# Where one vector engine runs its convolution taps: spread over the steps of prompt attention and over other pages of the cached sequences

## What is computed

```python
z = rms_norm(x) @ w_in                       # q latent | kv latent | rotary key | conv input
# group B: latent attention, 8 heads; prompt causal, samples over 16 cached pages + own tokens
# group A: convolution over time, 512 channels, 31 taps
glu = a * jax.nn.sigmoid(g)
xc = jnp.concatenate([conv_state, glu], axis=1)
y = depthwise_conv(xc, conv_w) + conv_b      # y[t, c] = sum_k xc[t + k, c] * w[k, c]
y = silu(layer_norm(y))
x = x + concat(rms_norm(attn), rms_norm(y)) @ w_out
x = x + (silu(h @ w_gate) * (h @ w_up)) @ w_down          # h = rms_norm(x), width 2816
x = x + sigmoid(rms_norm(x) @ w_ple_gate) * (p @ w_ple_proj)
```

## Time and profile before

| | us |
|---|---|
| median of 3 runs (1737.22 to 1741.24) | 1740.86 |
| the profiled execution | 1738.36 |
| its span, first to last instruction | 1736.3 |
| PE busy | 1654.8 |
| DVE busy | 1243.3 |
| ACT busy | 660.2 |
| POOL busy | 525.1 |

### The profile page before, as it was taken

One profiled execution on the slowest core, in us unless ns is written; L12 is line 12 of the kernel. 1 busy time (PEld: TensorE's weight loads), 2 busy tenths in 40 slices (PEclk: granted clock), 3 DMA queues, 4 the chain that ended last, 5 costly groups with the idle time before them and its releaser, 6 DMA issues.

```text
span 1736.3 us, 28852 instructions
## 1 busy us (share of the span) xinstructions
PE 1654.8 (95%) x10632; PEld 1480.8 (85%) x10632; DVE 1243.3 (72%) x1843; ACT 660.2 (38%) x1240; POOL 525.1 (30%) x351
## 2 busy tenths in 40 slices
PE   6999898999999999989998999999999999999998
PEld 6999787677788898877888999999999888887886
DVE  5385887776689889876689777777777577955444
ACT  5302345664444444553443223233222244542111
POOL 2204585420465565541124222222221000700000
PEclk9999999999999999999999999999999999999999
DMA  6401000001242222302103444444444877662011
GB/s 185 148 1 47 15 1 1 1 1 51 60 132 68 67 58 57 89 21 84 49 25 107 166 149 142 140 140 140 140 140 141 285 241 273 200 215 79 31 44 46
DMA packets 156044, 172.89 MB, mean 100 GB/s; under 512 B 35155, under 2 KB 107376, under 8 KB 155805
## 3 DMA queue, kind: packets, MB, share of 16 engines
q1 hardware_dynamic: 153939, 170.52, 30.7%
q10 hardware_dynamic: 2002, 1.03, 0.2%
HBM read 131.06 MB, written 40.80 MB: 99 GB/s over the span
## 4 chain that ended last, share of the span: by engine, by line
PE 74%; DVE 10%; POOL 5%; issue 4%; ACT 3%; SPq 3%; DMA 1%; ACTq 0%; DVEq 0%; POOLq 0%
PE ps L2619 20%; PE ps L2621 20%; PE ps L2620 20%; POOL stats L976 2%; PE ps L3034 2%; PE ps L2860 1%; SPq L761 1%; DVE arena L2184 1%; PE ps L2817 1%; PE ps L616 1%; DVE arena L1789 1%; PE ps L2922 1%; PE ps L2813 1%; PE ps L2819 1%; PE ps L2818 1%
## 5 line engine op out<-in xcount | busy, mean ns | idle before, releaser
L1125 POOL TENSOR_TENSOR arena<-arena,mhalf 128x32 f32<-128x32 f32 x32 | 176.4, 5512 | 130.2 <-DVE arena L2188 130.2
L2619 PE MATMUL ps<-cw_hi,pT_hi 128*128 128x288 f32 x512 | 161.8, 316 | 9.9 <-DVE pT_lo L2076 5.6
L1789 DVE SCALAR_TENSOR_TENSOR arena<-arena,tapw 128x1024 f32<-128x1024 f32 x120 | 161.8, 1348 | 1.5
L2393 DVE TENSOR_TENSOR dn_lo<-dn_raw,dn_hi 128x1024 fp32r<-128x1024 f32 x83 | 116.8, 1416 | 61.6 <-ACT dn_hi L1692 60.7
L2619 PE MATMUL ps<-T_hi,S_hi 128*128 128x272 f32 x528 | 152.7, 289 | 3.7 <-DVE F_B_r L670 1.8
L2620 PE MATMUL ps<-F_B_r,S_hi 128*128 128x272 f32 x528 | 152.3, 288 | 0.0
L2621 PE MATMUL ps<-T_hi,S_lo 128*128 128x272 f32 x528 | 152.0, 288 | 0.0
L2620 PE MATMUL ps<-cw_lo,pT_hi 128*128 128x288 f32 x512 | 150.8, 294 | 0.0
L2621 PE MATMUL ps<-cw_hi,pT_lo 128*128 128x288 f32 x512 | 150.7, 294 | 0.0
L1692 ACT ACTIVATE dn_hi<-dn_raw 128x1024 fp32r<-128x1024 f32 x83 | 87.6, 1060 | 136.0 <-DMA dn_raw<-in_w_down 66.7
L1440 ACT ACTIVATE arena<-ps 128x512 f32<-128x512 f32 x128 | 76.7, 599 | 123.8 <-PE ps L2621 123.7
(11 more groups left out here) (403 smaller groups left out, 4852.7 us busy)
## 6 DMA issues: line engine op xcount, KB each, us to landing
dn_raw<-act_mid SPq DMA_DIRECT2D x77, 256.0 KB, 2.7
arena<-in_cache_ckv SPq DMA_DIRECT2D x128, 128.0 KB, 2.0
dn_raw<-in_w_down SPq DMA_DIRECT2D x45, 256.0 KB, 3.5
w_raw<-in_w_gate SPq DMA_DIRECT2D x22, 512.0 KB, 4.0
w_raw<-in_w_up SPq DMA_DIRECT2D x22, 512.0 KB, 5.3
arena<-in_w_down SPq DMA_DIRECT2D x22, 512.0 KB, 5.8
act_mid<-arena SPq DMA_DIRECT2D x11, 1024.0 KB, 7.6
wt_mid<-arena SPq DMA_DIRECT2D x11, 1024.0 KB, 4.4
```

What stands on the lines that cost most here:

```text
L1125: nc.gpsimd.tensor_tensor(rstd_k[:, 4 * q:4 * q + 4, :], ms_k[:, 4 * q:4 * q + 4, :], mhalf[:, 0:4 * NH].rearrange("p (g h) -> p g h", h=N ...
L1789: ins = nc.vector.scalar_tensor_tensor(y_of(c), glu[:, c, k:k + SEQ], tapw[:, c, k:k + 1], y_of(c), ALU.mult, ALU.add)
L2393: nc.vector.tensor_tensor(dn_lo_r[s], dn_raw[s], dn_hi[s][0], ALU.subtract).then_inc(s_("a_split"), 1)
L2619: mm(out, left[0], right[0], start=start, stop=False)
```

## The change

Four edits, all in the order of instructions; none is added or removed.

- DVE, prompt attention: the `taps(4)` at the start of steps 8, 16 and 24 go. In steps 1 to 6 of each pair's eight, one tap is taken after the second row maximum. The `taps(4)` behind the last step stays.
- DVE, cached sequences: a tap in pages 0, 1, 2, 4, 6, 8, 10 and 14 instead of in each of pages 6 to 14.
- SP: the rope pages of sequence 1 are issued right behind those of sequence 0, ahead of the wait for the end of the prompt's outputs, of the own rows and of sequence 1's latent pages.
- PE and ACT: chunk 0 of the convolution is turned and copied before the sample rows of the convolution are, which wait for the last output scaling. The counts of `yT_done` follow.

```diff
+TAP_PAGES = (0, 1, 2, 4, 6, 8, 10, 14)
@@ SP
             load_kpe(0, 0)
+            load_kpe(1, 1)
             sp.wait_ge(s_("o_evac"), NH)
             load_own(1)
             load_ckv(1, 1)
-            load_kpe(1, 1)
@@ ACT
             def chunk_copy(c):
-                act.wait_ge(s_("yT_done"), c + 2)
+                act.wait_ge(s_("yT_done"), c + 1 if c == 0 else c + 2)
...
             high_pair(0)
-            act.wait_ge(s_("yT_done"), 1)
+            chunk_copy(0)
+            act.wait_ge(s_("yT_done"), 2)
             nc.scalar.activation(conv_tok[0:NS, TILES, :], ps[0:NS, O_BANK, :], ACT.Copy).then_inc(s_("yT_ready"), 1)
-            chunk_copy(0)
@@ DVE, prompt attention
                 if first:
-                    taps(4)
                     out_rows(2 * (k // TILES) - 2)
                 if k + 1 < STEPS:
                     row_max(0, k + 1)
                 if k + 2 < STEPS:
                     row_max(1, k + 2)
+                if 1 <= k % TILES < TILES - 1:
+                    taps(1)
@@ DVE, cached sequences
-                    if 6 <= g < NPAGE - 1:
+                    if g in TAP_PAGES:
                         taps(1)
@@ PE
             out_T(NH - 1)
+            chunk_T(-1, 0)
             pe.wait_ge(s_("ys_summed"), 4 * CCH)
             pe.wait_ge(s_("o_evac"), NH)
...
             last.then_inc(s_("yT_done"), 1)
-            chunk_T(-1, 0)
```

## The result

The changed kernel took 1747.45 us (median of 6 runs, 1744.87 to 1747.95), the kernel before 1739.84 on the same chip: ratio 1.0033, 95% interval 1.0022 to 1.0044. The profiled execution went from 1738.36 to 1747.95 us, its span from 1736.3 to 1745.9. Lines of the changed file stand one or two lower: L1790 is the tap, L1976 the row maximum, L1992 and L1997 the wide and the short copy, L2031 the column maximum, L2066 the last quad's scores, L2862 the weighted sum, L3036 `pv`.

A forecast was written before the change was run, and what follows sets the result against it. PE, busy for 95% of the span, was taken to bound the kernel. Attention +7.0, cached sequences with the rope +4.4 and the swap 0 gave +11.4 on 1738.4, so 1749.8 us; range 1739 to 1763.

The forecast's parts named there:

- Attention: Four head pairs of prompt attention: taps in the steps cost 2.0 + 1.75 + 1.75 + 1.5 = +7.0 us, kept at 2 to 14.
- the lock: Pair 0: a tap starting under a GpSimd subtract waits for the port pair VectorE and GpSimd share; 1.0 us added.
- The walk: Pair 2's steps followed through DVE's queue: scores start 0.4, 1.1, 1.3, 1.7 and 1.75 us late; 1.75 taken.
- Pair 3: Last head pair of prompt attention: no scores ahead in its last two steps, so its taps cost 1.5 us.
- The bursts at zero: Attention: the bursts of four taps lay under PE's weighted sums, so taking them away gives 0.
- Rival 3: Clock: more idle time in the steps, more low-clock stretches or subtract hits in pair 0; +5 to +8, about 1756; chance 0.14.
- Cached sequences with the rope: Cached stage: waits on low parts, issue and rope pages go, -9.1; taps ahead of page 5's work add +13.5; sum +4.4 us.
- The stand-in of sequence 7: Sequence 7's w_out work on pages 0, 1 and 4 costs PE 1.4 us; one more tap makes 2.7 per sequence.
- Rope pages and swap: Start of cached stage: the 1.8 us rope wait goes, latent pages come in time; the swap gives 0, at most 0.9.
- the steps swallow their taps: Rival for attention: DVE's idle time takes in six taps a pair; attention +0, sequences +4.4, 1743 us; chance 0.14.
- nothing shows: Rival for the whole change: work only moves between covers; 1738 to 1741 us; chance 0.04.
- The faster case: Rival: spreading works in both stages, all 9.1 us gained and nothing paid, decided at L2029 by page 5; 1729.3; chance 0.10.

The follow-up runs named there:

- no_bursts: other_pages without the three attention bursts of four taps, the twelve taps moved into the cached sequences; 1740.66 us, ratio 0.9995 to the kernel before.
- no_step30: The changed kernel without the tap of step 30, left to the sequences instead; 1751.97 us, ratio 1.0070 to the kernel before.
- two_moved: The changed kernel with the taps of pages 1 and 2 moved to pages 7 and 9; 1739.68 us, ratio 0.9986 to the kernel before.
- rope_swap_alone: The kernel before with only the rope pages ahead and chunk 0 turned first, no tap moved; 1739.09 us, ratio 0.9981.
- pair0_bare: other_pages with step taps in place of the bursts, in pairs 1 to 3 only; 1735.62 us, ratio 0.9969 to the kernel before.
- other_pages: Kernel before with rope pages and swap as changed, bursts kept, nine taps a sequence on pages 0, 6 to 10, 13, 14; 1726.73 us, ratio 0.9908.
- steps_alone: The kernel before with only the attention taps moved into the steps; 1745.52 us, ratio 1.0015.
- other_again: The same kernel as other_pages, measured once more in a later series; 1732.90 us, ratio 0.9956 to the kernel before.

## Why the prediction came out right, step by step

The forecast was +11.4 us on the profiled execution; it is +9.6 (1747.95 against 1738.36), of which 8.6 in the stretch. By medians of the same series it is +7.6. The mechanism held in both stages: taps queued ahead of work that PE waits for. That the total came so near is partly luck, for the errors cancel. In the attention the clock gave back 3.0 us in pairs 1 and 3 and took 1.5 in pair 0; in the sequences both terms were too small, by 4.0 us of gain and 2.3 of cost.

**Attention, predicted +7.0, measured +5.8.** The step holds, the terms differ. At like clock the four pairs are 1.55 + 1.45 + 1.05 + about 3.3, some 7.3 us (an estimate, with the fall of the clock in pair 3 put at 1.5).
- Pair 0: predicted 2.0, half of it the lock. At like clock it is 1.55, which two stretched taps (1.47 together) about fill, where the prediction had one such tap and 1.0 of overload; the profile's 3.08 has 1.5 us of clock in it.
- Pair 1: predicted 1.75. At like clock 38.12 - 36.67 (pair 1 of no_bursts) = 1.45. It shows as -0.05 because before had the clock fall in this pair and after had not.
- Pair 2: predicted 1.75 and 38.4 us, measured 1.05 and 37.69. The walk was right for two steps (0.4 and 1.1 us late, measured 0.43 and 1.04) and too steep after them: it had 1.3, 1.7 and 1.75, and the scores stayed 1.04 late. One of the six taps is the `tensor_scalar` that begins a chunk, 0.81 us instead of 1.28, which I had not looked up. It can explain up to 0.5 of the missing 0.7; but the full tap ahead of it had already added nothing. The waits for the wide and short copies that the prediction named as a sign came to 0.25 us.
- Pair 3: predicted 1.5 as the smallest, measured 1.76, and about 3.3 if the fall of before (1.5) is put back, an estimate. This is the attention's term that was most mis-sized. "Pair 3 has no scores ahead in its last two steps" took it for the less critical pair; without scores of its own to do PE comes to the short transposes early and waits 1.82 us for the copy behind the tap, 1.2 of which no_step30 gives back.
- The bursts at zero: shown by no_bursts.
- Rival 3 had more falls of the clock in the pairs. The reverse came: the six profiles with no taps in the steps of pairs 1 to 3 have a fall in two of these three pairs each, 12 of 18. The seven with step taps in all pairs have none in 21; three of them have one just behind the wait of 1.83 or 1.10 us at the end of pair 3, and their unload takes 15.23 us instead of 13.55. In the changed kernel that is 3.0 us won that the sum did not have. Why the step taps keep the clock up in the pairs no run shows.

**Cached sequences with the rope, predicted -9.1 + 13.5 = +4.4, measured -1.71 + 4.44 = +2.7.** Both terms were too small.
- What goes: 13.1 us instead of 9.1. A period is 39.36 before and 37.06 (38.33 with a chunk) without stall, 9.6 for the six periods; the first page to the first `pv` takes 53.1 in two_moved and 56.65 before, 3.5 with the rope wait. The sum took only what the profile lists as waits. The rest is in short gaps, and in PE's busy time, 37.63 us before and 36.93 in the unstalled period for the same matmuls.
- What comes: 15.8 us instead of 13.5. The stand-in of sequence 7 and one tap more gave 2.7 of waiting in each of five sequences. Measured are 2.0 to 2.2. The six periods carry 14.0 over the unstalled ones: 8.4 of waits (1.99, 2.15, 2.07 and 2.15 in sequences 2 to 5), three falls of the clock, put at the 1.5 that one cost in pair 2, 4.5, and the 1.1 that is left, which I take for short gaps. Sequence 1 has 1.96 of waits and a fall of its own, seen against two_moved as 1.8.
- So the waits were over-sized by a quarter, and the clock behind them was missing. Rival 3 had the mechanism and put it in the wrong stage.

**Rope pages and swap: right.** -1.8 predicted, -1.76 measured in rope_swap_alone. (The -1.71 of the changed kernel's row, first page to first `pv`, is another sum: 3.5 won with the rope wait and the low parts, 1.8 lost at page 5 and to the clock.) The swap gave nothing, because the wait of 0.48 for GpSimd's low weights became 1.34. The latent pages came in time: no wait for them.

**The rivals.** That the steps swallow their taps is out (pair0_bare, no_bursts and pair 2), and so is "nothing shows". The faster case, that the spreading of the taps works, decides at the page-5 chain as the prediction said, and with this set of pages it fails there. Its mechanism is real all the same: with pages 1, 2 and 4 left out, other_pages keeps nearly the whole gain (37.28 us a period against 37.06 without a stall).

## What to carry to other kernels

Free time of an engine doesn't come in a sum but in gaps. For each place where work is put, follow the queue behind it to the next instruction that another engine waits for; at a place where that one had 0.05 us of slack, the first tap of 1.28 us cost no waiting all the same, the second 0.8 us and the third 1.4, while nine taps at places with room cost 0.2 us together. Then read the clock of the stretch beside its waits, since a stall of 2 us can cost 3.5. And compare profiles between the same instructions, not by their spans, when the effect is smaller than the spread of the rest.

## What the runs showed of the hardware that I had not expected

The granted clock falls behind short waits, and not behind all of them. Behind waits of 1.39 and 0.76 us inside 2.2 us it fell for part of two 4-us windows (0.88 and 0.69), and behind the same kind of stall at 541 (0.71, 0.77, 0.51) it did not, nor behind 1.38 and 0.77 in sequence 5 of no_step30. At the first steps of a pair the same two waits, 0.80 and 0.61, come in every kernel in each of pairs 1 to 3; a fall followed in two pairs of three without step taps, and in one of 24 with them (pair 1 of pair0_bare). At the end of pair 3 a wait of 1.82 or 1.83 us came in six kernels and one of 1.10 in a seventh; a fall followed in three of the seven and cost 1.7 us (15.23 instead of 13.55). Which it will be stays open.

The clock can also stay low while PE has work without a break, by its records. In steps_alone pair 0 ran at half speed through six windows, with PE busy for 4.00 of 4.00 us in each; two of them:

```profile
288.00:292.00 4.00, 4.00 (x25) 3.23 (x24) 2.34 (x4) 2.50 (x3) 0.39 (x2) 0.51 0.00 0
308.00:312.00 4.00, 4.00 (x14) 2.83 (x12) 1.09 (x1) 0.00 (x0) 0.00 (x0) 0.51 0.00 0
```

That is 1.2 GHz instead of 2.4 for 24 us, and pair 0 took 48.08 us instead of 41.34. The changed kernel has it in a smaller form (0.54 and 0.60 at 296 to 304). The spread of a kernel's own times goes with this clock: other_again took 1728.37 us at a mean granted clock of 0.992 and 1740.44 at 0.986.
